# Triangular inverse by halves of a bank: the product of matrix and inverse is carried, two products a level in place of three

## What is computed

```python
def wkv7_scan(r, w, k, v, kk, a, s0, reverse, emit):
    def step(S, inp):
        r_t, w_t, k_t, v_t, kk_t, a_t = inp
        sa = jnp.einsum('bhvk,bhk->bhv', S, -kk_t)
        S = (S * w_t[:, :, None, :] + sa[..., None] * (kk_t * a_t)[:, :, None, :]
             + v_t[..., None] * k_t[:, :, None, :])
        y = jnp.einsum('bhvk,bhk->bhv', S, r_t) if emit else None
        return S, y
```

```python
    g_rwkv, g_mla = jnp.split(jax.nn.sigmoid(p_gate + P['gate_b']), N_BRANCH, axis=-1)
    merged = g_rwkv * (y_rwkv @ P['w_rwkv_proj']) + g_mla * (o @ P['w_mla_proj'])
```

## Time and profile before

| | us |
|---|---|
| median of three runs | 4133.12 |
| lowest and highest | 4129.96, 4136.05 |
| the profiled execution's own time | 4133.48 |
| its span | 4131.8 |
| PE busy in it | 3881.2 (94%) |
| DVE busy, ACT busy | 2504.3, 1733.5 |

### The profile page before, as it was taken

How to read it: one execution, slowest core, us unless ns; L and a number is a source line. 1 busy time by engine, 2 the same in 40 slices (tenths; PEclk the granted TensorE clock), 3 DMA queues, 4 the chain that set the end, 5 groups by cost and what they waited for, 6 DMA issues and landing times.

```text
span 4131.8 us, 86832 instructions
## 1 busy us (share of the span) xinstructions
PE 3881.2 (94%) x36296; PEld 3297.9 (80%) x36296; DVE 2504.3 (61%) x4412; ACT 1733.5 (42%) x3153; POOL 273.9 (7%) x437
## 2 busy tenths in 40 slices
PE   6999999688998999998999999999999999899999
PEld 3778878466666799997999999977778678787879
DVE  2544588555555567577878777764452553646465
ACT  2544323333342345445444444452343342534354
POOL 0000011222222200000000000000000000000000
PEclk8999999799998999999999999999999999999999
DMA  9422566455555577574666666632223232433335
GB/s 364 149 72 66 206 206 197 131 172 162 176 174 169 160 253 233 186 233 139 214 217 217 215 218 207 215 124 85 77 62 97 67 113 97 129 121 90 120 95 186
DMA packets 289441, 662.43 MB, mean 160 GB/s; under 512 B 21088, under 2 KB 31328, under 8 KB 287536
## 3 DMA queue, kind: packets, MB, share of 16 engines
q1 hardware_dynamic: 233392, 441.74, 33.4%
q0 software_dynamic: 55680, 215.34, 16.7%
HBM read 639.17 MB, written 17.83 MB: 159 GB/s over the span
## 4 chain that ended last, share of the span: by engine, by line
PE 81%; DVE 11%; ACT 3%; issue 3%; DMA 2%; SPq 0%; POOL 0%; DVEq 0%; ACTq 0%; POOLq 0%
PE psum L860 61%; PE psum L825 3%; PE psum L1127 2%; PE psum L1139 1%; DVE wlo L2179 1%; PE psum L884 1%; ACT whi L1548 1%; PE psum L840 1%; PE psum L1052 1%; DVE smx L2918 1%; DMA ada_head<-in_w_ada 1%; PE psum L1449 1%; PE psum L1166 1%; PE psum L1143 1%; PE psum L1116 1%
## 5 line engine op out<-in xcount | busy, mean ns | idle before, releaser
L2179 DVE TENSOR_TENSOR wlo<-raw,whi 128x512 fp32r<-128x512 f32 (+3 forms) x1568 | 1054.0, 681 | 1044.8 <-ACT whi L1548 1036.1
L1548 ACT ACTIVATE whi<-raw 128x512 fp32r<-128x512 f32 (+3 forms) x1568 | 970.1, 623 | 1513.8 <-PE psum L860 1484.8
L860 PE MATMUL psum<-hhi,whi 128*128 128x512 f32 (+1 forms) x2416 | 835.9, 346 | 54.9 <-DVE wlo L2179 21.1
L860 PE MATMUL psum<-hlo,whi 128*128 128x512 f32 (+1 forms) x2416 | 816.2, 338 | 0.0
L860 PE MATMUL psum<-hhi,wlo 128*128 128x512 f32 (+1 forms) x2416 | 815.8, 338 | 0.0
L860 PEld LDWEIGHTS psum<-hhi,whi 128*128 128x128 f32 x2416 | 465.6, 193 | 150.2 <-issue 62.0
L860 PEld LDWEIGHTS psum<-hhi,wlo 128*128 128x128 f32 x2416 | 465.6, 193 | 47.6
L860 PEld LDWEIGHTS psum<-hlo,whi 128*128 128x128 f32 x2416 | 466.1, 193 | 46.6 <-issue 2.2
L860 PE MATMUL psum<-fhi,whi 128*128 128x256 f32 x1408 | 401.6, 285 | 19.8 <-DVE wlo L2179 15.3
L860 PE MATMUL psum<-flo,whi 128*128 128x256 f32 x1408 | 400.3, 284 | 0.0
L860 PE MATMUL psum<-fhi,wlo 128*128 128x256 f32 x1408 | 400.3, 284 | 0.0
(11 more groups left out here) (429 smaller groups left out, 7042.4 us busy)
## 6 DMA issues: line engine op xcount, KB each, us to landing
raw<-in_w_in SPq DMA_DIRECT2D x328, 512.0 KB, 3.8
ada_raw<-in_w_ada POOLq DMA_DIRECT2D x192, 512.0 KB, 4.4
red_raw<-in_w_adaT POOLq DMA_DIRECT2D x128, 512.0 KB, 4.4
raw<-in_w_out SPq DMA_DIRECT2D x96, 512.0 KB, 3.6
raw<-in_w_gate SPq DMA_DIRECT2D x88, 512.0 KB, 4.0
raw<-in_w_val SPq DMA_DIRECT2D x88, 512.0 KB, 4.3
raw<-in_w_down SPq DMA_DIRECT2D x88, 512.0 KB, 4.3
ada_head<-in_w_ada SPq DMA_DIRECT2D x64, 512.0 KB, 10.1
```

The lines of the kernel that those rows point to most:

```text
L860: mm = pe.matmul(dst, l, r, start=(k == 0 and i == 0 and first), stop=(k == nch - 1 and i == 2), skip_group_check=True)
L1548: act.activation(whi[:, lc % HL, 0:width], raw[:, (lc // 2) % RAW, lc % 2, 0:width], ACT.Copy).then_inc(w_hi, 1)
L2179: dve.tensor_tensor(wlo[:, lc % HL, 0:width], raw[:, (lc // 2) % RAW, lc % 2, 0:width], whi[:, lc % HL, 0:width].bitcast(F32), ALU.subtrac ...
```

## The change

Four things are changed together.

1. The inverse. `xinv`, `yinv`, `bm` and `aT` give way to `yz` (inverse Y and product Z = A·Y side by side, 128 columns) and `el` (the masked part of Z, transposed). Each step multiplies `el` with [Y Z], 128 columns wide, and Z with `el`. All products of a step read and write the same half `HS[1-e]`, but for the last. There are six steps: one full one for Z alone (`first_level`), three in two halves of four blocks (`half_level`, since Y and Z of eight blocks would fill two banks), `fourth_level`, and `last_level` with one product.
2. Banks by turns. The blocks of gates, `rproj` and `mproj` use banks 0 to 3 and 4 to 7 in turn, and a block waits for the block before the last (`back=4`).
3. The order of POOL's loads after the pairs: `cond_l` first, then eight `red_raw` after the gates' eighth chunk, then `oT`.
4. ACT's copies and DVE's masks follow the new steps; `key_directions` and `mask_keys(1)` move by a few places on DVE.

```diff
+                def first_level(d):
+
+                    if d == 1:
+                        dve_at("I1")
                     for g in range(8):
                         for e in range(2):
+                            q = HS[1 - e]
+                            pe.matmul(PS[2 * d][q, ch(g)], el[d][q, g, :], yz[d][q, g, 64:P], start=True, stop=True)
+                        for e in range(2):
+                            q = HS[1 - e]
+                            mm = pe.matmul(PS[2 * d + 1][q, ch(g)], yz[d][q, g, 64:P], el[d][q, g, :], start=True, stop=True)
+                    done(mm, f"G{d}0")
+
+                def half_level(d, s, half):
+
+                    if half == "a":
+                        act_at(f"C{d}0" if s == 1 else f"C{d}{s - 1}b")
+                        dve_at(f"M{d}1" if s == 1 else f"M{d}{s}b")
+                    else:
+                        act_at(f"C{d}{s}a")
+                        dve_at(f"M{d}{s + 1}a")
+                    for g in range(4 if half == "b" else 0, 8 if half == "b" else 4):
+                        for e in range(2):
+                            q = HS[1 - e]
+                            pe.matmul(PS[2 * d][q, blk(g % 4)], el[d][q, g, :], yz[d][q, g, :], start=True, stop=True)
+                        for e in range(2):
+                            q = HS[1 - e]
+                            mm = pe.matmul(PS[2 * d + 1][q, ch(g)], yz[d][q, g, 64:P], el[d][q, g, :], start=True, stop=True)
+                    done(mm, f"G{d}{s}{half}")
...
-                def y_out(d, l):
-                    pe_at(f"Y{d}{l}")
-                    done(act.activation(yinv[d][:, :, :], g8(2 * d + 1), ACT.Copy), f"Y{d}{l}")
+                def half_out(d, s, half):
+                    pe_at(f"G{d}{s}{half}")
+                    g = 4 if half == "b" else 0
+                    done(act.activation(yz[d][:, g:g + 4, :], b4(2 * d), ACT.Copy), f"C{d}{s}{half}")
...
+                def level(d, s, half=""):
+
+                    pe_at(f"G{d}{s - 1}{half}")
+                    g = slice(4 if half == "b" else 0, 4 if half == "a" else 8)
+                    n = g.stop - g.start
+                    done(TT(el[d][:, g, :], PS[2 * d + 1][:, :].rearrange("p (g c) -> p g c", c=CH)[:, g, :],
+                            m64((M_LEVEL_T if d else M_LEVEL) + s).unsqueeze(1).to_broadcast([P, n, CH]), ALU.mult), f"M{d}{s}{half}")
...
-                            pe.wait_ge(blk_free, b0 + m - 3)
+                            pe.wait_ge(blk_free, b0 + m - 3 - back)
...
             for it in range(1, 8):
-                seg(C0["gate"] + it * 16, 0, 16, B0["gate"] + it * 4, 4, h1)
+                if it == 1:
+                    pe.wait_ge(rw_dve, RW_END)
+                    pe.wait_ge(rw_act, RW_ACT_END + 1)
+                seg(C0["gate"] + it * 16, 0, 16, B0["gate"] + it * 4, 4, h1_far if it % 2 else h1, back=4)
...
-                x_ = rows(lambda k: xh[:, k, :], lambda k: xl[:, k, :], TOK)
                 for it in range(4):
-                    seg(C0[name] + it * n, 0, n, B0[name] + it * 4, 4, x_, parts=split)
+                    x_ = rows(lambda k: xh[:, k, :], lambda k: xl[:, k, :], TOK, bank=it % 2 * 4)
+                    seg(C0[name] + it * n, 0, n, B0[name] + it * 4, 4, x_, parts=split, back=4)
...
             pool.wait_ge(rw_dve, RW_END)
-            pool.dma_start(oT[:, :, :], o_keep).then_inc(o_in, 16)
-            pool.wait_ge(ada_used, 8 * (ADA_HEAD + 24))
-            reduce_in(RED_EARLY, RED_EARLY + 4)
             pool.wait_ge(s_lo, 4)
             pool.dma_start(cond_l[:, :, :], cond_keep).then_inc(cond_in2, 16)
+            pool.wait_ge(ada_used, 8 * (ADA_HEAD + 24))
+            pool.wait_ge(w_used, C0["gate"] + 8)
+            reduce_in(RED_EARLY, RED_EARLY + 4 + 2 * RED_GATE)
+            pool.wait_ge(cond_in2, 16)
+            pool.dma_start(oT[:, :, :], o_keep).then_inc(o_in, 16)
+            reduce_in(RED_EARLY + 4 + 2 * RED_GATE, RED_EARLY + 7 * RED_GATE + 4)
             pool.wait_ge(o_in, 16)
-            reduce_in(RED_EARLY + 4, RED_EARLY + 7 * RED_GATE + 4)
-            pool.wait_ge(cond_in2, 16)
```

More of the change, by code:

```diff
@@ L283, in build @@
         k_tok = [sb(f"k_tok{d}", [P, 4, P], D0 + 10 + 4 * d) for d in range(2)]
[L284 to L287, removed]
+        yz = [sb(f"yz{d}", [P, 8, P], D0 + 32 + 8 * d) for d in range(2)]
+        el = [sb(f"el{d}", [P, 8, CH], D0 + 38 + 8 * d) for d in range(2)]
         hd = [sb("hd0", [P, 8, CH], D0 + 124.5), sb("hd1", [P, 8, CH], D0 + 40)]
@@ L842, in ada_final, with seg @@
                 mm.then_inc(ada_fin, 1)
-            def seg(c0, lc0, nch, b0, nblk, product, each=True, ready=None, between=None, parts=None):
+            def seg(c0, lc0, nch, b0, nblk, product, each=True, ready=None, between=None, parts=None, back=0):
                 for k in range(nch):
@@ L876, in _ @@
             h1 = rows(lambda k: hhi[:, 1, k, :], lambda k: hlo[:, 1, k, :], TOK)
+            h1_far = rows(lambda k: hhi[:, 1, k, :], lambda k: hlo[:, 1, k, :], TOK, bank=4)
             def total(n, j, of, src, bank=5, squares=None):
@@ new lines, in fourth_level @@
+                def fourth_level(d):
+                    act_at(f"C{d}3b")
+                    dve_at(f"M{d}4b")
+                    for g in range(8):
+                        for e in range(2):
+                            q = HS[1 - e]
+                            pe.matmul(PS[2 * d][q, ch(g)], el[d][q, g, :], yz[d][q, g, 0:64], start=True, stop=True)
+                        for e in range(2):
+                            q = HS[1 - e]
+                            mm = pe.matmul(PS[2 * d + 1][q, ch(g)], yz[d][q, g, 64:P], el[d][q, g, :], start=True, stop=True)
+                    done(mm, f"G{d}4")
@@ L1146, in from_values, with last_level @@
+                def last_level(d):
+                    act_at(f"C{d}4")
+                    dve_at(f"M{d}5")
+                    for g in range(8):
+                        for e in range(2):
+                            mm = pe.matmul(PS[2 * d][HS[e], ch(g)], el[d][HS[1 - e], g, :], yz[d][HS[1 - e], g, 0:64], start=True, stop=True)
+                    done(mm, f"G{d}5")
                 def from_values(d):
@@ L1200, in _ @@
                 chunk_pairs(done, 1)
-                level_b(0, 1)
+                first_level(0)
                 act_at("v")
@@ L1204, in _ @@
                 ada(0, 1)
-                level_b(1, 1)
-                level_xy(0, 1)
+                first_level(1)
+                half_level(0, 1, "a")
                 act_at("ta0")
@@ L1209, in _ @@
                 ada(0, 2)
-                level_xy(1, 1)
+                half_level(1, 1, "a")
                 dve_at("ar0")
@@ L1223, in _ @@
                 ada(0, 5)
-                level_xy(1, 2)
+                half_level(1, 2, "a")
                 act_at("tk0")
@@ L1227, in _ @@
                 ada(0, 6)
-                level_b(0, 3)
+                half_level(0, 2, "b")
                 def kn_ready():
@@ L1234, in _ @@
                 ada(0, 7)
-                level_b(1, 3)
+                half_level(1, 2, "b")
                 act_at("sd")
@@ L1260, in _ @@
                 ada(1, 5)
-                level_b(0, 5)
+                last_level(0)
                 key_norms_out(done, act_at)
-                level_b(1, 5)
                 ada(1, 6)
+                last_level(1)
                 from_values(1)
                 ada(1, 7)
-                level_xy(0, 5)
                 ada_final(it * 3 + ADA_HEAD + 1, 0)
@@ L1878, in _ @@
                 values_out(0)
+                y_out(0, 5)
                 values_out(1)
+                y_out(1, 5)
                 ada_take(it * 3 + ADA_HEAD + 1)
[L1881 to L1882 removed]
                 pe_at("g")
```

143 lines of the change are left out of this document (65 added, 78 removed).

## The result

The changed kernel takes 4165.16 us (median of 4 runs, 4160.95 to 4171.33), the kernel before 4134.59 in the same comparison (4129.96 to 4139.33). The ratio is 1.0076 with a 95% interval of 1.0061 to 1.0091: 0.76% slower, 31 us. The profiled execution took 4163.73 us, with a span of 4162.1 where it was 4131.8 before, so the two traces differ by 30.3 us.

What follows compares the result with a forecast made beforehand. PE was taken as the bound, holding 81% of the chain. Pairs +41, loads -9, `oT` +0.5 and banks -10.5 gave +22 on 4133.5, so 4155 us, range 4138 to 4170.

Steps and rivals of the forecast that it cites:

- the forecast case: Whole kernel: the expected outcome, 4155 us with its own range 4145 to 4165; chance 0.62.
- What PE pays for a step: Inverse: products of one quarter of the array follow each other, so a pair takes 28.1 us, 6.3 more than before.
- the rival of the records: Inverse: the count of records sets the price, 704 for 896, -37 us for eight pairs, total 4077; chance 0.07.
- The page of the Trainium skill with its fixed overhead per matmul: Inverse: about 60 cycles per matmul would make it cheaper by an estimated 4.8 us a pair; the prediction disagreed.
- What covers it: Pairs, first level to `solve`: only 0.94 us goes into the `start_inverse` wait, no new waits; net +5.2 us a pair.
- The sign that the prediction named for itself: Trace after, first level to `solve`: stretches of 55 to 56 us with no new PE wait.
- small savings that I put at 0.2 us a pair: Pairs: savings in other drains, taken as 0.2 us a pair in reaching net +5.2.
- The rival of the new round trips: Half steps: PE waits for a copy and a mask of the half before, +8 us, total 4163; chance 0.12.
- The clock: Levels of the inverse: half the array at rest might lower the clock; a tenth of +225 is +22, 4177; chance 0.03.
- The pairs: Eight pairs, first level to `solve`: +41 us, ends +36 and +50; the stretch from `solve` on keeps its lengths.
- The loads: Behind the pairs: waits of 5.5 and 3.0 us and half a us go, -9; `oT` in the gates costs 0.5.
- Banks by turns: `rproj` and `mproj` block boundaries: 5.2 and 6.8 us of waits go, less 1.5 for DVE, -10.5; nothing in the gates.

Runs made afterwards that it cites:

- `four_quarters`: Changed kernel, but each step's second product goes to the other half of the partitions and DVE's mask brings it back in two operations; 4102.78 us, ratio 0.9930.
- `loads_alone`: Kernel before with only the new order of POOL's loads; 4124.83 us, ratio 0.9978 to the kernel before.
- `banks_alone`: Kernel before with only the alternating use of banks 0 to 3 and 4 to 7; 4115.68 us, ratio 0.9966 to the kernel before.
- `four_quarters_one_mask`: As `four_quarters`, but DVE's mask stays one operation that doesn't cross, so the result is not the inverse; 4099.82 us, ratio 0.9926 to the kernel before.

## Why the prediction was right, and where it was off

The forecast was 4155 us, 4138 to 4170, slower. The median is 4165, in the range and above the forecast case's own 4145 to 4165 by a hair. That it is no farther off is in part luck: the pairs grew by 54 us, outside the bounds of 36 to 50 that I gave them, and gains that came out 3.7 us larger made up for a part. By its steps:

**What PE pays for a step: right.** Predicted were 1.48 us for a half step and 2.02 for a full one; the trace has 1.49 (in ten of a pair's twelve; the first two are a little shorter) and 1.92 to 2.01. `four_quarters` shows that the reason is the right one, and takes the rival of the records away. The page of the Trainium skill with its fixed overhead per matmul ("TensorEngine Tiling (Array Packing)", Instruction Overhead) didn't forecast this either: the records became fewer and the time longer. Under Key Properties the same page of the Trainium skill says that different tiles work in parallel; the traces agree, and show the other side, that products of one tile follow each other.

**What covers it: the step that failed.** "I walked through the new order with these durations, looking for waits" and found none. I had walked through the steps of the inverse only, and those are indeed without a wait. But a product taken out of level 5 had been the cover of another chain, the skinny product's last step, copy, selection and sum. That is 1.77 us a pair, 14.1 us. The sign that the prediction named for itself, stretches of 55 to 56 us with no new wait of PE, did not come: they take 56.3 to 57.8 with two new waits. Against it stand small savings that I put at 0.2 us a pair: the earlier trace rows's wait shrank by 8.3 us and not 7.5, and the third pair's 6.14 leaves 1.0 us for short waits that the longer steps fill (6.3 less 0.94 plus 1.77 would be 7.1). Two of them stand in the groups at 951.10 and 954.82 of the kernel before, which take 1.44 and 1.61 us where others of their kind take 1.08 and 1.10. The rival of the new round trips, one us a pair on ACT and DVE, is nearest to what happened, though the round trip is not one of the inverse.

**The clock: a rival that I placed wrongly.** I gave it 0.03 and looked for it in the half-empty array of the levels. They run at 1.00. It fell at the two new waits and cost 6.0 us in the stretches and 6.4 directly behind them. In the sum of the stretches this hides, because the first pair before was 4.7 us longer than the third, with 3.4 us of waits put down to issue and a clock of 0.97, and that is not so after.

**The pairs: +41 forecast, +54 measured.** The stretches +49.0, behind `solve` +2.7, and 2.2 ahead of them.

**The loads: right, undersized.** −8.5 forecast, −11.7 measured; `loads_alone` has 10.0. The two waits of 8.5 us went, and with them a spell of lower clock behind them (0.97 on average in the gates before, 0.99 after). `oT` in its new place holds up nothing: no wait of PE in the gates is for it.

**Banks by turns: right.** −10.5 forecast, −11.0 measured (4.5 and 6.5 where 5.2 and 6.8 less 1.5 were the terms). The sentence that nothing is won in the gates was wrong by 2.2 us in `banks_alone`.

So 13 us too few in the pairs and 3.7 too few in the gains behind them made the forecast 8 us low in the traces (+22 for +30.3; the 0.9 that the two leave over lies behind `mproj`).

## What to carry to other kernels

Count small matmuls by the quarter of the array that they sit in, not by their number: products in one quarter follow each other, and here a cheap change was to send a result to the other half of the partitions. When a product is taken out of a hand-written order, list every chain that ran beside it, not only its own, and put other work into the place. Gaps of one us can also cost what the clock loses behind them: here taking away 14 us of waits gave 26.

## What the runs showed of the hardware

- A mask on DVE can read PSUM in one half of the partitions and write SBUF in the other. An operation of 64 partitions takes as long as one of 128 with the same number of columns (0.69 us for 512, 0.42 for 256), so crossing in two operations doubles DVE's time for it.
- Two products with rows in different halves write to the same PSUM bank, in different partitions, side by side: the two wide products of a block, four records, take 0.22 us in the changed kernel (973.22 to 973.44), the time of two records of one quarter at 0.109.
- Two PE waits of 0.9 us, 2.5 us apart, came with a granted clock of 0.50, for 3.4 to 6.8 us, in six of eight places of the changed kernel, six of eight of `four_quarters` and four of eight of `four_quarters_one_mask`; one wait of 0.5 us with none in eight.
- The first stretch of the old inverse lost 3.4 us to waits that the profile puts down to issue (2.5 to 3.1 in the three other kernels that have it), that of the carried product 0.4 at most. It has 192 records fewer; that this is the reason was not tried.
